# Last mixer of a three-mixer transformer kernel: mask of the picked keys in PSUM, another spacing of the convolution taps, three value products a head

## What is computed

```python
u_conv, q, k, v, q_idx, k_idx, w_idx, gates = jnp.split(h @ w_in[l], split_at, axis=-1)
...
y_a = conformer_conv_branch(u_conv, ...)        # a * sigmoid(gate), depthwise conv of 31 taps, layer norm, silu
y_b = dsa_sparse_attention(q, k, v, q_idx, k_idx, w_idx, attn_w_o[l])
stream = stream + (g_a * y_a + g_b * y_b) @ w_merge_out[l]
...
# in dsa_sparse_attention, for a block of queries
score = einsum("bqh,bqhs->bqs", wb, relu(dots))  # an index score of each key
score = where(is_meta, META_BONUS, where(visible, score, -inf))
vals, idx = lax.top_k(score, top_k)              # top_k is 68 here
p = softmax(q . k[idx]);  o = p @ v[idx]
```

## Time and profile before

| | |
|---|---|
| median of 3 runs | 1148.07 us (1147.68 to 1149.96) |
| the profiled execution, its own time | 1148.63 us |
| its span, from the first to the last instruction | 1146.8 us |
| PE busy | 96% |
| DVE busy | 66% |
| ACT busy | 50% |
| POOL busy | 19% |
| mean granted clock of PE | 0.981 |
| the last mixer, slots 0 to 399 | about 650 to 862 us of the span |

### The profile page before, as it was taken

How to read it: one execution, slowest core, us unless ns; L and a number is a source line. 1 busy time by engine, 2 the same in 40 slices (tenths; PEclk the granted TensorE clock), 3 DMA queues, 4 the chain that set the end, 5 groups by cost and what they waited for, 6 DMA issues and landing times.

```text
span 1146.8 us, 22301 instructions
## 1 busy us (share of the span) xinstructions
PE 1098.3 (96%) x8813; PEld 1071.1 (93%) x8813; DVE 751.3 (66%) x1232; ACT 576.0 (50%) x840; POOL 214.8 (19%) x198
## 2 busy tenths in 40 slices
PE   7998999999999999999999899988999889999998
PEld 7996999999999999999999799987999889999997
DVE  6766565555667776565555457998775657788753
ACT  5666554443554555444454434434656446655542
POOL 1432030001131111100000167773440000000000
PEclk9999999999999999999999899997999999999999
DMA  8734256656775343565456344451335443555460
GB/s 262 213 121 136 65 178 189 202 162 198 237 225 172 119 145 99 187 195 184 146 178 207 111 147 148 147 161 61 111 110 185 143 151 126 168 183 172 139 203 37
DMA packets 187925, 181.36 MB, mean 158 GB/s; under 512 B 17935, under 2 KB 186268, under 8 KB 187851
## 3 DMA queue, kind: packets, MB, share of 16 engines
q1 hardware_dynamic: 187323, 178.23, 49.1%
q0 software_dynamic: 528, 2.10, 0.6%
HBM read 179.27 MB, written 1.05 MB: 157 GB/s over the span
## 4 chain that ended last, share of the span: by engine, by line
PE 82%; DVE 8%; ACT 5%; POOL 3%; issue 2%; DMA 0%; SPq 0%; ACTq 0%; POOLq 0%; DVEq 0%
PE ps L547 25%; PE ps L548 24%; PE ps L549 24%; DVE ps L2488 2%; ACT w_hi L370 2%; POOL work L473 2%; POOL w_lo L398 1%; PE ps L2014 1%; PE ps L2039 1%; PE ps L456 1%; PE ps L2040 1%; PE ps L1896 1%; DVE gates L2550 1%; PE ps L1903 0%; DVE top L2546 0%
## 5 line engine op out<-in xcount | busy, mean ns | idle before, releaser
L547 PE MATMUL ps<-u_hi,w_hi 128*128 128x256 f32 (+2 forms) x1800 | 518.0, 288 | 14.3 <-DVE u_lo L516 6.9
L548 PE MATMUL ps<-u_lo,w_hi 128*128 128x256 f32 (+2 forms) x1800 | 511.6, 284 | 0.0
L549 PE MATMUL ps<-u_hi,w_lo 128*128 128x256 f32 (+2 forms) x1800 | 510.7, 284 | 0.0
L386 DVE TENSOR_TENSOR w_lo<-raw,w_hi 128x2048 fp32r<-128x2048 f32 (+3 forms) x157 | 326.5, 2090 | 147.4 <-ACT w_hi L370 147.0
L547 PEld LDWEIGHTS ps<-u_hi,w_hi 128*128 128x128 f32 x1800 | 343.8, 191 | 17.2 <-issue 13.0
L548 PEld LDWEIGHTS ps<-u_lo,w_hi 128*128 128x128 f32 x1800 | 343.5, 191 | 0.7
L549 PEld LDWEIGHTS ps<-u_hi,w_lo 128*128 128x128 f32 x1800 | 344.1, 191 | 0.0
L370 ACT ACTIVATE w_hi<-raw 128x2048 fp32r<-128x2048 f32 (+3 forms) x182 | 316.4, 1753 | 39.4 <-PE ps L549 29.1
L547 PE MATMUL ps<-a_hi,w_hi 128*128 128x256 f32 x528 | 146.0, 276 | 0.0
L548 PE MATMUL ps<-a_lo,w_hi 128*128 128x256 f32 x528 | 145.9, 276 | 0.0
L549 PE MATMUL ps<-a_hi,w_lo 128*128 128x256 f32 x528 | 145.8, 276 | 0.0
(11 more groups left out here) (327 smaller groups left out, 1321.8 us busy)
## 6 DMA issues: line engine op xcount, KB each, us to landing
raw<-in_w_in SPq DMA_DIRECT2D x24, 1024.0 KB, 5.4
raw<-in_w_gate SPq DMA_DIRECT2D x22, 1024.0 KB, 5.3
raw<-in_w_up SPq DMA_DIRECT2D x22, 1024.0 KB, 5.4
raw<-in_ffn_up SPq DMA_DIRECT2D x22, 1024.0 KB, 5.1
raw<-in_w_down SPq DMA_DIRECT2D x16, 768.0 KB, 4.4
raw<-in_od_w_qkv SPq DMA_DIRECT2D x12, 1024.0 KB, 5.3
raw<-in_w_down SPq DMA_DIRECT2D x16, 640.0 KB, 4.4
raw<-in_ev_w_in SPq DMA_DIRECT2D x7, 1024.0 KB, 10.4
```

What stands on the lines that cost most here:

```text
L386: nc.vector.tensor_tensor(w_lo[t % RING][:, 0:n], raw[t % RAW][:, 0:n], w_hi[t % RING][:, 0:n].bitcast(F32), ALU.subtract).then_inc(lo_don ...
L547: nc.tensor.matmul(out_ap, a_h, b_h, start=start and n == 0, stop=False)
L548: nc.tensor.matmul(out_ap, a_h, b_l, start=False, stop=False)
L549: mm = nc.tensor.matmul(out_ap, a_l, b_h, start=False, stop=stop and n == len(pairs) - 1)
```

## The change

Three things change, all in the last mixer.

**The mask.** `above` and `equal` now lie in PSUM banks 3 and 4, which hold index scores earlier and attention scores later. The number of higher keys is now the start value of the running count of equal keys, so the separate subtraction from 68 is gone, and the rest is done with one operation over all 416 columns at a time, the last one writing `pick` itself. 16 instructions become 13 (the listing below shows a repeated one as x2), and seven points at which DVE waits for itself become five.

**The taps.** `conv_due` becomes every third slot in 36 to 135, every sixteenth in 136 to 271, and stays at every second from 272 on. `first_tokens` moves from slot 246 to slot 310.

**The values.** The transposed meta rows of a head are copied twice by ACT, scaled with `half_rows`, to `pt_meta`, and `v_meta` exists once, unscaled. Both query blocks lie side by side, so that a head has three products instead of five. `pt_meta` has one buffer: ACT's copy of head n waits for the values of head n-1 (before, with two buffers, of head n-2).

```diff
-    PICK_AT, COLS_AT = 238, 246
+    PICK_AT, COLS_AT = 238, 310
...
-        if 36 <= x < 136 or 236 <= x < 272:
-            return x % 4 == 0
-        if 136 <= x < 236:
-            return x % 8 == 0
+        if 36 <= x < 136:
+            return x % 3 == 0
+        if 136 <= x < 272:
+            return x % 16 == 0
         return x >= 272 and x % 2 == 0
...
         def dsa_copies(n):
             act.wait_ge(sem("dsa_pt"), n + 1)
-            wait(act, sem("dsa_o"), n - 1)
-            nc.scalar.activation(pt4[:, n % 2, 0:3 * P], ps[:, 5, 0:3 * P], ACT.Copy)
-            nc.scalar.activation(pt4[0:2 * META, n % 2, 3 * P:], ps[0:2 * META, 5, 3 * P:], ACT.Copy).then_inc(sem("dsa_ptc"), 1)
+            wait(act, sem("dsa_o"), n)
+            nc.scalar.activation(pt4[:, n % 2, :], ps[:, 5, 0:3 * P], ACT.Copy)
+            for b in range(2):
+                a = nc.scalar.activation(pt_meta[:, b, :], ps[0:2 * META, 5, 3 * P:], ACT.Copy,
+                                         scale=c("half_rows")[0:2 * META, b:b + 1])
+            a.then_inc(sem("dsa_ptc"), 1)
...
-            for b, tokens in enumerate(((0,), (0, 1))):
-                o = ps[:, 6, b * P:(b + 1) * P]
-                for m, v in enumerate(tokens):
-                    at = (b + m) * P
-                    nc.tensor.matmul(o, v_d[:, v, dh], own[:, at:at + P], start=m == 0, stop=False)
-                mm = nc.tensor.matmul(o, v_meta[:, b, dh], own[0:2 * META, 3 * P:], start=False, stop=True)
+            o = ps[:, 6, 0:T1]
+            nc.tensor.matmul(o, v_d[:, 0, dh], own[:, 0:2 * P], start=True, stop=False)
+            nc.tensor.matmul(o[:, P:], v_d[:, 1, dh], own[:, 2 * P:], start=False, stop=False)
+            mm = nc.tensor.matmul(o, v_meta[:, dh], pt_meta[:].rearrange("p b n -> p (b n)"), start=False, stop=True)
...
-            for t in range(2):
-                mix_released(dve, mix_tile("cv", 3, t))
             last = (TOPK - 1) % 8
+            above, equal = idx_bank(0), idx_bank(1)
             for b, (lo, hi) in enumerate(DSA_SPANS):
                 thr = top8[:, b, last:last + 1]
                 nc.vector.tensor_scalar(above[:, lo:hi], acc[:, lo:hi], thr, None, ALU.is_gt)
                 a = nc.vector.tensor_scalar(equal[:, lo:hi], acc[:, lo:hi], thr, None, ALU.is_equal)
             link(a)
             for b, (lo, hi) in enumerate(DSA_SPANS):
-                nc.vector.reduce_sum(need[:, b:b + 1], above[:, lo:hi], AX)
-                a = nc.vector.tensor_tensor_scan(left[:, lo:hi], wide_ones[:, 0:hi - lo], equal[:, lo:hi], 0.0, ALU.mult, ALU.add)
+                a = nc.vector.reduce_sum(need[:, b:b + 1], above[:, lo:hi], AX)
             link(a)
-            link(nc.vector.tensor_scalar(need[:], need[:], -1.0, float(TOPK), ALU.mult, ALU.add))
             for b, (lo, hi) in enumerate(DSA_SPANS):
-                a = nc.vector.scalar_tensor_tensor(out=left[:, lo:hi], in0=left[:, lo:hi], scalar=need[:, b:b + 1],
-                                                   in1=equal[:, lo:hi], op0=ALU.is_le, op1=ALU.mult)
+                a = nc.vector.tensor_tensor_scan(left[:, lo:hi], wide_ones[:, 0:hi - lo], equal[:, lo:hi], need[:, b:b + 1],
+                                                 ALU.mult, ALU.add)
             link(a)
-            link(nc.vector.tensor_tensor(left, left, above, ALU.add))
-            link(nc.vector.tensor_scalar(left, left, -NEG, NEG, ALU.mult, ALU.add))
+            link(nc.vector.scalar_tensor_tensor(out=left, in0=left, scalar=float(TOPK), in1=equal, op0=ALU.is_le, op1=ALU.mult))
+            link(nc.vector.scalar_tensor_tensor(out=above, in0=above, scalar=-1.0, in1=left, op0=ALU.add, op1=ALU.add))
             for lo, hi in unseen:
-                a = nc.vector.tensor_tensor(left[:, lo:hi], left[:, lo:hi], c("seen_mask"), ALU.add)
-            link(a)
-            nc.vector.tensor_copy(pick[:], left).then_inc(sem("pick_ready"), 1)
+                nc.vector.scalar_tensor_tensor(out=pick[:, lo:hi], in0=above[:, lo:hi], scalar=-NEG, in1=c("seen_mask"),
+                                               op0=ALU.mult, op1=ALU.add)
+            lo, hi = unseen[0][1], unseen[1][0]
+            nc.vector.tensor_scalar(pick[:, lo:hi], above[:, lo:hi], -NEG, None, ALU.mult).then_inc(sem("pick_ready"), 1)
```

More of the change, by code:

```diff
@@ L251, in build @@
             p4 = sb("p4", [P, 2, P + META + T2], scope=t)
-            pt4 = sb("pt4", [P, 2, 4 * P], scope=t)
+            pt4 = sb("pt4", [P, 2, 3 * P], scope=t)
         sb("rope_place", [P, 2 * KEYS + 4 * T2], scope=s)
@@ L262, in build @@
             u_twice = sb("u_twice", [P, 2, KT, 2 * META], F32R, scope=t)
-        v_meta = sb("v_meta", [2 * META, 2, KVH * DH], scope=s)
+        v_meta = sb("v_meta", [2 * META, KVH * DH], scope=s)
+        pt_meta = sb("pt_meta", [2 * META, 2, P], scope=s)
         wi = sb("wi", [P, 2, IH], scope=s)
@@ L290, in build @@
     acc, left = picks[:, 0:416], picks[:, 416:832]
-    sg_flat = sg4[:].rearrange("p a b c -> p (a b c)")
-    def dots(n):
-        return sg_flat[:, n * 416:(n + 1) * 416]
-    above, equal = dots(0), dots(1)
     ps = ctx.enter_context(nc.psum_tensor("ps", [P, 8, 512], F32))
@@ L1482, in mix_evicted @@
                 if t == 0:
-                    for b in range(2):
-                        a = nc.scalar.activation(v_meta[:, b, :], ps[0:2 * META, T % 3, UC:2 * UC], ACT.Copy,
-                                                 scale=c("half_rows")[0:2 * META, b:b + 1])
-                    a.then_inc(read, 1)
+                    nc.scalar.activation(v_meta[:], ps[0:2 * META, T % 3, UC:2 * UC], ACT.Copy).then_inc(read, 1)
             else:
@@ L2056, in meta_step @@
                 for g in range(KVH):
-                    mm = nc.tensor.matmul(ps[:, 6, 64:64 + META], v_meta[:, g, g * DH:(g + 1) * DH], meta_pt[:],
-                                          start=g == 0, stop=g == KVH - 1)
+                    own = slice(g * META // 2, (g + 1) * META // 2)
+                    mm = nc.tensor.matmul(ps[:, 6, 64 + own.start:64 + own.stop], v_meta[:, g * DH:(g + 1) * DH], meta_pt[:, own],
+                                          start=True, stop=True)
                 mm.then_inc(sem("meta_o"), 1)
```

## The result

| | before | changed |
|---|---|---|
| time, us (median; lowest to highest) | 1149.01 (1147.68 to 1151.50) | 1133.85 (1133.53 to 1134.13) |
| span of the profiled execution, us | 1146.8 | 1131.7 |

The ratio is 0.9863, with a 95% interval from 0.9848 to 0.9877: 15.2 us less. The forecast was 1130.8 us with a range from 1128.8 to 1134.2. The time lies inside the range, 3 us over the forecast; the gain is 15.2 us where 17.3 were expected, and the other 0.9 us is the median of the kernel before, which was 1148.07 when the forecast was made and is 1149.01 here. Measured twice more beside the experiments, the changed kernel took 1134.75 and 1135.43 us (before: 1148.49 and 1148.98), ratios 0.9872 (0.9826 to 0.9918) and 0.9888 (0.9868 to 0.9908).

A forecast was written before the change was run, and what follows sets the result against it. PE, busy 96% of the span, was taken as the bound, held up by a late DVE in the last mixer. Gains of 12.5 + 4.8 = 17.3 us against the median of 1148.07 gave 1130.8 us, range 1128.8 to 1134.2.

The forecast's parts named there:

- What bounds the kernel: PE, busy 96% of the span; in the last mixer it waits twice for a late DVE and runs at half clock.
- part 2: PE's gain around the mask: both waits gone and the clock no longer falling, 12.5 us.
- Both waits and the half-clock stretch: Last mixer: PE idle 4.45 us for `rope_cos` and 4.49 for `q_first`, clock 0.50 from 774.3 to 786.5.
- Part 1: DVE's mask: fewer taps ahead let it start near 758.2, 5.3 us of instructions end it near 763.5 instead of 773.1.
- Rival (a): The mask still waits for POOL in all its steps: gain 10.2 us, so 1138; chance 0.08.
- Rival (b): DVE's load moves to slots 36 to 135 and PE stops there: costs 3 us, 1134; chance 0.07.
- (d): A head's softmax chain outgrows PE's ten slots: slower, 1152 if it grows by 3.5 us; chance 0.03.
- (e): Another wait, for instance for weights, replaces the two at once: 1143; chance 0.02.
- late `p`: Sign of being wrong: PE shows a new wait for `p` before the transposes.
- Part 3: Value products of the eight heads: three cost about 1.1 us instead of 1.68, 0.6 less a head, 4.8 in all.
- rival (c): Wide value products cost the upper price, 0.51 us for 256 columns, 1.34 a head: 1133; chance 0.08.
- The cover of the extra copy: ACT's extra copy, at most 0.4 us, lies beside PE; a softmax's cover before its transposes falls from 1.85 to 0.85.

The follow-up runs named there:

- values alone: The kernel before with only the three value products a head and their copies; mask, taps and `first_tokens` as before: 1147.76 us, ratio 0.9978.
- tap slots alone: The kernel before with only the new tap slots and `first_tokens` at slot 310: 1144.80 us, ratio 0.9951.

## Why the prediction was right, and where it was not

- **What bounds the kernel, and part 2** held. 12.5 us were forecast, 12.59 measured between the marks. Both waits and the half-clock stretch went, and nothing came in their place. The spare time that I gave to the first wait, 4.9 us, and to the second, 2.4, was about right: the experiments give 5.2 and 2.8.
- **Part 1** held step by step. PE's stream to this place ran 1.3 us earlier in the changed kernel's profile; add that, and the mask began at 758.2 (forecast 758.2) and ended at 763.5 (763.5). Its length was 5.4 us (5.3). Its instructions took 0.28 to 0.60 us, but for the running count of 272 columns, 0.75, which I had priced at 0.72 and left out of my 0.3 to 0.65.
- **Rival (a)**, POOL slowing the mask in PSUM, fell: the comparisons took 0.36 and 0.50 us in the middle of POOL's 10.23. The bound of 1.4 us each that I took from the SBUF form is what that form does in SBUF (1.38).
- **Rival (b)**: PE had no new wait before 760, and was busy for all of 690 to 758. The nine added steps cost nothing.
- **Rivals (d) and (e)** didn't come; the softmax chain kept its cover but at head 3 and, slightly, at the last head. At head 3 the transposes started 0.2 us late (799.91 + 0.12 = 800.03, and they start at 800.23), behind `first_tokens`, which POOL stretched. I had costed its move at nothing. The last head's start 0.18 us late with the new values, 0.08 with the old. These are small cases of the late `p` that I had named as a sign of being wrong.
- **Part 3 failed in size**: the step "one of 256 columns 0.34 by the two rotations of 258", and with it the meta product at 0.41 to 0.48. I read the rotations by start to start, 0.68 us for the two, but the `L547` behind them took 0.47 us where its kind takes 0.29. The 0.18 belongs to the rotations, and half of 0.86 is the 0.43 measured. The meta product took 0.62. Three products cost 1.37 us, not 1.1. That is rival (c), which had 1.34 and a chance of 0.08, and its 1133 is nearer to the measured time than my forecast; on the other side the five took 1.78, not the 1.68 of the chain, whose first row of 0.22 leaves out 0.1 of the first product. So 0.41 us a head: 3.3 in all, not 4.8.
- **The cover of the extra copy** was worked out for a head's softmax, where it held. It failed at a place I had not looked at: the wait for the meta tokens' values before head 0's, 0.64 us before, grew to 0.98, since the copy stands ahead of theirs on ACT. 3.3, less 0.3 here and 0.1 at the last head, is 2.9 (2.87 measured with the values alone), and less the 0.2 of head 3, 2.7 (2.63 measured).
- **The rest**: 12.59 + 2.63 = 15.2 is the difference of the medians. The forecast of 17.3 was 2.1 too high, all of it in part 3. The time inside the range is no luck of cancelled errors: the range was built from the prices of a wide product on either side, and the measured price lies at its upper end.

## What to carry to other kernels

When one engine is late ahead of a busy TensorE, price the lateness at the wait and at the slow clock behind it, and look for where the spare time ends rather than how many us were saved: 2.35 us more of DVE's work were free here, 6.6 cost 4.1. Where a bank is free, give what VectorE does beside GpSimd's work an operand in PSUM. Read the price of a matmul up to the point where the ones behind it are regular again. And look at the changes between weights of 32 and of 128 rows as well as at the number of products: here the rows put the larger part of the price there, though no run has tested it.

## What the runs showed of the hardware

- A scan with both of its tensors in SBUF is slowed by GpSimd as other two-input instructions are: the two took 2.43 us beside POOL and 1.18 with one tensor in PSUM; with both in SBUF they took 1.21 and 1.42 one by one beside POOL (tap slots alone) and 0.45 and 0.72 in POOL's gap (before).
- Two waits of 1.5 and 0.9 us, or one of 2.6, were enough to bring PE's clock from 2.4 to 1.2 GHz for part of the next 5 us; one of 1.0 us was not.
- Two fp32 products of 128 columns on the same weights cost what one of 256 does (0.63 and 0.62 us), but at each change between 32-row and 128-row weights the load had no head start over its product (four changes of four in the rows shown, against 0.21 us from `v_d` to `v_d`).
- The same instructions between two marks repeated to 0.01 or 0.02 us from one execution to the next, while the whole kernel moved by 2 us. An edit of 1.3 us was plain inside a trace, where the medians of four to six executions could not prove it.
